# The low half of most weight blocks is computed by GpSimd instead of VectorE, in a four-layer transformer kernel

## The reference

```python
x = x + ga1 * (mx @ w_out[i])                        # layers 0 and 1: after attention, pooling, Fourier
x = x + ga2 * swiglu(fx, w_gate_up[i], w_down[i])
...
px = hx @ w_in[i]                                    # layers 2 and 3
z = lax.conv_general_dilated(a * jax.nn.sigmoid(g), ...)   # 31 taps per channel
w = p1 - lam * p2                                    # two softmax maps per head, 8 heads
x = x + gx1 * ((g_conv * y_conv + g_attn * y_attn) @ w_out[i])
x = x + gx2 * (jnp.square(jax.nn.relu(h @ w1)) @ w2)
```

## Time and profile before

| what | value |
|---|---|
| timed runs | median 2640.07 us of 3 (2636.05 to 2645.23) |
| the profiled execution's own span | 2646.0 us |
| TensorE matmul busy | 2376.6 us, 90% |
| VectorE busy | 1424.6 us, 54% |
| ScalarE busy | 1082.0 us, 41% |
| GpSimd busy | 32.2 us, 1% |
| w_lo on VectorE | 444 instructions, 529.2 us |
| mean granted TensorE clock | 0.941 of full speed |

### The profile page before, as it was taken

How to read it: one execution, slowest core, us unless ns; L and a number is a source line. 1 busy time by engine, 2 the same in 40 slices (tenths; PEclk the granted TensorE clock), 3 DMA queues, 4 the chain that set the end, 5 groups by cost and what they waited for, 6 DMA issues and landing times.

```text
span 2646.0 us, 34404 instructions
## 1 busy us (share of the span) xinstructions
PE 2376.6 (90%) x13550; PEld 1873.4 (71%) x13550; DVE 1424.6 (54%) x2364; ACT 1082.0 (41%) x1826; POOL 32.2 (1%) x40
## 2 busy tenths in 40 slices
PE   5798999999878999879979899899998788989999
PEld 2355677777656888656548577588887666769899
DVE  4255433333655544798863634544434977656665
ACT  4153422212544333435564432423323455654543
POOL 0300000000010000000000000000000000000000
PEclk8898999999999999889989899899999898989999
DMA  6800444444314777325502122333222211225454
GB/s 258 292 33 32 144 143 144 145 135 141 132 46 160 261 248 241 118 80 191 187 24 92 48 74 91 114 103 104 91 92 96 80 64 44 96 69 182 150 183 146
DMA packets 94879, 335.87 MB, mean 127 GB/s; under 512 B 10624, under 2 KB 12672, under 8 KB 94464
## 3 DMA queue, kind: packets, MB, share of 16 engines
q1 hardware_dynamic: 94720, 333.67, 37.2%
HBM read 332.58 MB, written 1.05 MB: 126 GB/s over the span
## 4 chain that ended last, share of the span: by engine, by line
PE 71%; DVE 15%; ACT 6%; DMA 4%; issue 3%; SPq 0%; ACTq 0%; DVEq 0%
PE out L996 21%; PE out L997 20%; PE out L998 20%; DMA raw<-stream 4%; DVE stage L1557 3%; PE sc L976 2%; DVE w_lo L1322 2%; PE pv L1073 2%; PE aux L1006 2%; PE sc L1051 1%; DVE smax L1506 1%; PE pt L1061 1%; ACT w_hi L1107 1%; ACT e_t L1228 1%; DVE rs L1449 1%
## 5 line engine op out<-in xcount | busy, mean ns | idle before, releaser
L996 PE MATMUL out<-act_hi,w_lo 128*128 128x512 f32 (+1 forms) x2272 | 814.4, 358 | 58.3 <-DVE act_lo L1460 46.0
L997 PE MATMUL out<-act_lo,w_hi 128*128 128x512 f32 (+1 forms) x2272 | 793.6, 349 | 0.0
L998 PE MATMUL out<-act_hi,w_hi 128*128 128x512 f32 (+1 forms) x2272 | 792.0, 349 | 0.0
L1107 ACT CAST w_hi<-raw 128x1024 fp32r<-128x1024 f32 (+2 forms) x444 | 452.6, 1021 | 494.3 <-PE out L998 433.1
L1322 DVE TENSOR_TENSOR w_lo<-raw,w_hi 128x1024 fp32r<-128x1024 f32 (+2 forms) x444 | 529.2, 1197 | 199.7 <-ACT w_hi L1107 199.3
L996 PEld LDWEIGHTS out<-act_hi,w_lo 128*128 128x128 f32 x2272 | 443.6, 195 | 149.7 <-issue 87.1
L998 PEld LDWEIGHTS out<-act_hi,w_hi 128*128 128x128 f32 x2272 | 442.1, 195 | 52.9
L997 PEld LDWEIGHTS out<-act_lo,w_hi 128*128 128x128 f32 x2272 | 443.9, 195 | 50.3 <-issue 0.5
L996 PE MATMUL out<-mix_hi,w_lo 128*128 128x256 f32 (+1 forms) x1184 | 403.0, 340 | 4.1 <-DVE mix_lo L1344 2.1
L997 PE MATMUL out<-mix_lo,w_hi 128*128 128x256 f32 (+1 forms) x1184 | 398.9, 337 | 0.0
L998 PE MATMUL out<-mix_hi,w_hi 128*128 128x256 f32 (+1 forms) x1184 | 398.5, 337 | 0.0
(11 more groups left out here) (146 smaller groups left out, 1784.4 us busy)
## 6 DMA issues: line engine op xcount, KB each, us to landing
raw<-stream SPq DMA_DIRECT2D x604, 512.0 KB, 3.8
raw<-stream SPq DMA_DIRECT2D x16, 384.0 KB, 4.1
raw<-stream SPq DMA_DIRECT2D x16, 256.0 KB, 3.0
x<-xin SPq DMA_DIRECT2D x1, 2048.0 KB, 11.6
consts<-const SPq DMA_DIRECT2D x1, 1344.0 KB, 8.3
x<-ctx SPq DMA_DIRECT2D x1, 1024.0 KB, 5.7
out<-x SPq DMA_DIRECT2D x8, 128.0 KB, 1.7
consts<-const SPq DMA_DIRECT2D x1, 320.0 KB, 11.4
```

The costliest lines, as they stand in the source:

```text
L996: nc.tensor.matmul(ps, wl, xh, start=(k == 0), stop=False)
L997: nc.tensor.matmul(ps, wh, xl, start=False, stop=False)
L998: ins = nc.tensor.matmul(ps, wh, xh, start=False, stop=(k == s.nk - 1))
L1107: nc.scalar.copy(w_hi[:, number % HL, 0:n], raw[:, place[number] % RAW, 0:n]).then_inc(S["hi_ready"], 1)
```

## The change

Each block gets a maker of its w_lo, by a rule: VectorE keeps it for the blocks near the pooling windows of layers 0 and 1, for the first three blocks, and for the even blocks of layers 1 and 3; GpSimd gets all others. With layers counted from 0, GpSimd then has 76 of the 86 blocks of layer 0, 38 of 86 in layer 1, all 136 in layer 2 and 68 of 136 in layer 3, 318 in all. The semaphore lo_ready becomes two, lo_dve and lo_pool, each with its own count, and SyncE and TensorE wait for the one that belongs to the block. On GpSimd the subtraction for block number + 3 comes at each step wb, behind a wait for hi_ready; it is the same instruction with the same operands. After the windows GpSimd waits for their last instruction.

```diff
-        names = """wb_done out_act out_dve hi_ready lo_ready ada_used ...
+        names = """wb_done out_act out_dve hi_ready lo_dve lo_pool ada_used ...
...
+        lo_by, lo_at = [], []
+        lo_count = {"lo_dve": 0, "lo_pool": 0}
+        for s in steps:
+            if s.kind == "wb":
+                mat = blocks[s.number][0]
+                near_windows = s.layer < 2 and mat in ("w_k", "w_v", "w_pl", "w_fr", "w_q")
+                on_dve = near_windows or s.number < AHEAD or (s.layer % 2 == 1 and s.number % 2 == 0)
+                name = "lo_dve" if on_dve else "lo_pool"
+                lo_count[name] += 1
+                lo_by.append(name)
+                lo_at.append(lo_count[name])
+
+        def wait_lo(eng, number):
+            eng.wait_ge(S[lo_by[number]], lo_at[number])
...
-                        sp.wait_ge(S["lo_ready"], before[1] + 1)
+                        wait_lo(sp, before[1])
...
-                    pe.wait_ge(S["lo_ready"], group[-1].number + 1)
+                    for g in group:
+                        wait_lo(pe, g.number)
...
+            def split_lo(number):
+                if number >= last_block or lo_by[number] != "lo_pool":
+                    return
+                pool.wait_ge(S["hi_ready"], number + 1)
+                n = blocks[number][3] * P
+                nc.gpsimd.tensor_tensor(w_lo[:, number % HL, 0:n], raw[:, place[number] % RAW, 0:n],
+                                        w_hi[:, number % HL, 0:n].bitcast(F32), ALU.subtract).then_inc(S["lo_pool"], 1)
+
             for s in steps:
+                if s.kind == "wb":
+                    split_lo(s.number + AHEAD)
                 if s.kind != "windows":
                     continue
...
+                pool.wait_ge(S["windows_done"], s.done[1])
...
-                if number >= last_block:
+                if number >= last_block or lo_by[number] != "lo_dve":
                     return
                 dve.wait_ge(S["hi_ready"], number + 1)
```

More of the change, by code:

```diff
@@ L888, in col @@
             return vecs[:, a:a + n]
-        names = """wb_done out_act out_dve hi_ready lo_ready ada_used mods_read mods_ready square_done square_added
+        names = """wb_done out_act out_dve hi_ready lo_dve lo_pool ada_used mods_read mods_ready square_done square_added
             aux_ready aux_read guess_ready rstd_done xn_ready xh_ready act_ready qk_ready windows_done pt_ready pt_read
@@ L1322, in split_lo @@
                 nc.vector.tensor_tensor(w_lo[:, number % HL, 0:n], raw[:, place[number] % RAW, 0:n],
-                                        w_hi[:, number % HL, 0:n].bitcast(F32), ALU.subtract).then_inc(S["lo_ready"], 1)
+                                        w_hi[:, number % HL, 0:n].bitcast(F32), ALU.subtract).then_inc(S["lo_dve"], 1)
             due = []
```

## The result

The changed kernel takes 2674.7 us in the median of 4 runs (2671.8 to 2677.7) beside 2640.7 for the kernel before (4 runs, 2636.1 to 2645.2). The ratio is 1.013, with a 95% interval of 1.011 to 1.015. The forecast was 2639 us with a range of 2614 to 2658, so in effect no change. The change is a clear loss, and the time lies beyond even the far end of the slow rival (d), 2655 to 2670.

The account below looks back on a forecast made before the run. TensorE, busy 90% of the span, bounds the kernel, so only VectorE's stretches of the chain pay. Gains of 13.8 us, taken at two thirds (9.2), less costs of 8.1 net -1.1: 2639 us from the 2640.1 median, range 2614 to 2658.

Parts of the forecast that it names:

- rival (d): Slower: GpSimd holds the ports over 1.45 us; 26 collisions at 2.06 us give 2655, at 2.66 us 2670; chance 0.23.
- What bounds the kernel, and that the feed-forward of layer 2 is covered: TensorE busy 90% of the span, 351.2 of 352 us in layer 2's feed-forward, so nothing to gain there.
- Gross gain: Moved w_lo and freed waits on the chain, without any collisions: 37 us, two thirds of it 25.
- rival (b): Ports don't collide as read, or GpSimd's instruction lets VectorE in; nothing taken back: 25 us gained, 2615; chance 0.18.
- The mechanism of the cost: VectorE instructions with two SBUF inputs and GpSimd instructions take turns whole; VectorE loses 1.45 us per moved w_lo if queued.
- The head that the prediction walked through: Layer 2 attention: GpSimd gets in after the rstd pair; q_t waits 1.4 us where 1.14 us of w_lo has gone.
- The price of one collision: GpSimd's 128x1024 subtraction taken as 1.77 us from the windows' rows, holding VectorE 1.45 us without its fixed part.
- The holds in the forecast's sum: Collision costs in layer 2's attention, layer 3's start, the feed-forward changes of layer 3 and layer 1's alike.
- the taps' heads of layer 2 (blocks 180 to 201): 15 moved w_lo on the chain: eleven collisions +3.1 us, four freed waits -11.2, +1.5 taken back, together -6.6.
- the four changes: Layer 3 feed-forward, w_mlp1 to w_down: TensorE waits for the last mix_lo, which starts 1.45 us later; +5.8 us.
- the prediction's last sentence: What may have been missed: a delay of VectorE off the chain moves it onto the chain; no size given.
- (c): Freed wait behind w_hi is worth more: a fifth of 59.3 us turns into time, -12 us, 2627; chance 0.19.

Follow-up runs that it names:

- The narrow kernel: The kernel of experiment 1: the changed kernel, but GpSimd subtracts only 16 of up to 1024 columns of each of its blocks; 2610.7 us.
- experiments 1 to 3: Changed kernel with GpSimd's subtraction only 16 columns wide: 2610.7 us; as six 16-column subtractions: 2614.0; replaced by a memset: 2612.3; by a copy: 2626.2.
- 5 and 6: Changed kernel with four blocks given back to VectorE: 2664.6 us; changed kernel with each GpSimd subtraction cut into pieces of 256 columns: 2649.4 us.
- experiment 7: Kernel before with test additions, subtractions and a copy on GpSimd at its start; ran once; operands 1 or 2 elements apart faster by 0.46 us in 1024.
- experiment 1: Changed kernel, but GpSimd subtracts only 16 of up to 1024 columns per block, all waits and orders kept; 2610.7 us, ratio 0.988 to the kernel before.
- experiment 5: Changed kernel with blocks 391, 407, 423 and 439, at layer 3's changes from w_mlp1 to w_down, given back to VectorE; 2664.6 us, ratio 1.008.

## Why the prediction was wrong, by its own steps

**What bounds the kernel, and that the feed-forward of layer 2 is covered.** Right: 352 us before and after.

**Gross gain.** I had 37 us on the chain, of which rival (b) took two thirds, 25. The narrow kernel shows 31 us. The term was right within a quarter.

**The mechanism of the cost.** Right: experiments 1 to 3 show that POOL's reading holds up DVE's two-input instructions, and 5 and 6 agree with turns by whole instructions. The head that the prediction walked through, came out as it said but for the size. In the changed kernel, DVE first, then POOL:

```profile
1225.69 0.69 DVE L1478 SCALAR_TENSOR_TENSOR rs<-sq,rs 128x512 f32<-128x512 f32 x1
1226.42 2.74 DVE L1509 TENSOR_TENSOR q_t<-qg,rs 128x512 f32<-128x512 f32 x1
...
1225.95 2.66 POOL L1301 TENSOR_TENSOR w_lo<-raw,w_hi 128x1024 fp32r<-128x1024 f32 x1 [7.81 <-ACT w_hi L1125]
```

**The price of one collision: the first step that failed.** "I take 1.77, as the longest rows are the nearest in size" gave 1.45 us of hold. Measured is 2.05 (q_t 2.74 - 0.69; a held tap of 512 columns 2.76 to 2.88 instead of 0.75). The rows were nearest in size but not in kind (experiment 7). With 1.14 us saved per moved w_lo, 1.45 makes a collision nearly even and 2.05 makes it lose 0.9 us, so this one term turned the sign. The prediction's estimate from the Trainium skill ("GPSIMD Engine Reference", section "Elementwise — side-by-side cycle accounting"), 2.25 us, is near the measured 2.40, and its sentence "By that price each collision would cost about 0.5 us more and the change would be a loss." came true.

**Holds that the sum didn't count: the second step that failed.** The price alone doesn't give the size. The holds in the forecast's sum come to 31 us (15.6 + 1.5 + 1.6 + 5.4 + 5.8 + 1.4), and measured are 64, between experiment 1 and the changed kernel. Rival (d), with the right price, adds 16 to the 31. The other 17 us are holds that the sum took as free or did not have, and the low clock that follows them, at least the 3 us of experiment 5. These two steps make up 33 of the 36 us between 2639 and 2675. The clock's full share is open: in the traces PE is at the lower level for 306 us in the changed kernel, 271 in the narrow one, and 311 and 297 in the kernel before and that of experiment 7. As an estimate, at half speed the 35 us between the first two are at most 17 us of the 64.

**Stretch by stretch**, forecast and measured by position: the taps' heads of layer 2 (blocks 180 to 201) -6.6 and +5.4; from there to the last gates (201 to 220) -3.8 and -0.6; the start of layer 3 (308 to 319) +0.9 and +5.2; from there to the feed-forward (319 to 380) -3.4 and -1.0; the four changes +5.8 and +11.6; layer 1 up to the first block of layer 2 +1.4 and about +2. The places were right, and every size erred to the same side. For the four changes the parts are known: 4 x 2.15 of hold instead of 4 x 1.45, and 2 x 1.5 of low clock, which the sum had not. The measured numbers are of one execution each. The kernel of experiment 7, the same program as before in these places, is 2.0 us shorter in its trace than the kernel before from 319 to 380 and 2.4 in layer 1 (86 to 172), so against it the change loses about 1 us there, where a gain of 3.4 was forecast, and about 4 in layer 1; in the other stretches of the list it differs by 0.5 or less.

**What rival (d) still lacked.** It had 26 collisions at 2.06 us and 2655. Apart from small pieces it counted only those on the chain of before. The others were taken as free, and the prediction's last sentence named that as its weak point. One of them is seen in layer 3, where no w_lo was on the chain. DVE's timeline in the changed kernel, then POOL's:

```profile
2299.47 2.75 DVE L1509 TENSOR_TENSOR k_t<-qg,rs 128x512 f32<-128x512 f32 x1
2302.15 1.28 DVE L1351 TENSOR_TENSOR w_lo<-raw,w_hi 128x512 fp32r<-128x512 f32 x2
...
2299.24 2.44 POOL L1301 TENSOR_TENSOR w_lo<-raw,w_hi 128x1024 fp32r<-128x1024 f32 x1 [11.32 <-ACT w_hi L1125]
```

k_t is held up, and behind it in DVE's queue stands the w_lo of an even block, 338, which PE needs at once: it starts 2.4 us after the end of 337 (at 2302.92, and the first of the two w_lo in that row ends at 2302.82), and the block after it takes 4.16 us instead of 3.14, at a granted clock of 0.70 instead of 1.00. The stretch lost 3.35 us, 2.05 of them before 338 starts and the rest at the lower clock. How the rest of the difference between 2655 and 2675 divides between such places and the lower clock was not separated.

**Rivals (b) and (c).** (b), no turn-taking, is refuted by experiments 1 to 3. (c), the freed wait behind w_hi, is not needed: with hardly any hold left the whole gain was 31 us, against the 37 that the chain showed.

## What to carry to other kernels

Before moving two-input SBUF work from VectorE to GpSimd, look at what two-input SBUF work VectorE keeps beside it. A single short instruction behind GpSimd's waits for all of it, and where that one releases TensorE, four blocks of 318 cost 10 us here. A time that is added up from the positions of one trace carries that trace's own deviation, here some 7 us, as much as the effects that were looked for: hold it first against a trace with the same code in that place. Where such work must go to GpSimd, cut it into short pieces: here pieces of 256 columns took more GpSimd time and gave back 25 of 34 us. A price taken from a near row needs a row alike in operands, not only in size, and when the sign of the sum hangs on it, the forecast should stand at the worse end.

## What the runs showed of the hardware that was not expected

A two-input GpSimd instruction of 128x1024 took 1.89 us with its operands 1 or 2 elements apart in one tile and 2.35 us with an offset of 8 or in distant tiles, for addition and subtraction and for both output types. A GpSimd memset of 0.96 us beside VectorE's two-input instructions cost these nothing (mix_lo 419 ns), and a copy of 1.04 us cost 0.72. And a stall of TensorE of 2.4 us was followed in two of four places, the same two in two kernels' traces, by a block at a granted clock of 0.62, 1.5 us more.
